# Longer runs of weight products: a whole weight chunk per run where it was one output tile

## The reference, cut to what matters

```
h = x
layer 0: h += moba_nsa_mixer(rmsnorm(h)) @ w_out ;  h += relu(rmsnorm(h) @ w1)**2 @ w2
layer 1: h += fox_mixer(rmsnorm(h))     @ w_out ;  h += relu(rmsnorm(h) @ w1)**2 @ w2
h = rmsnorm(h)
h += 0.5*rmsnorm(swiglu(rmsnorm(h)))                 # ffn1, width 2816
h += rmsnorm([diff_attention, ssd_mixer] @ w_out_2)  # mixer
h += 0.5*rmsnorm(swiglu(rmsnorm(h)))                 # ffn2
```

## Time and profile before

| | us |
|---|---|
| median of 3 runs | 1223.89 (1222.49 to 1224.58) |
| profiled execution | 1224.94 |
| its span in the profile | 1223.1 |
| PE busy | 1189.3 (97%) |
| PEld busy | 1052.5 (86%) |
| DVE busy | 825.5 (67%) |
| ACT busy | 658.4 (54%) |
| POOL busy | 239.4 (20%) |

### The profile page before, as it was taken

One profiled execution on the slowest core, in us unless ns is written; L12 is line 12 of the kernel. 1 busy time (PEld: TensorE's weight loads), 2 busy tenths in 40 slices (PEclk: granted clock), 3 DMA queues, 4 the chain that ended last, 5 costly groups with the idle time before them and its releaser, 6 DMA issues.

```text
span 1223.1 us, 19217 instructions
## 1 busy us (share of the span) xinstructions
PE 1189.3 (97%) x7770; PEld 1052.5 (86%) x7770; DVE 825.5 (67%) x1267; ACT 658.4 (54%) x1074; POOL 239.4 (20%) x300
## 2 busy tenths in 40 slices
PE   6899999999999999999999999999999999999996
PEld 6786788888888788888888889999997799888996
DVE  6957776666586686666568776457965767777643
ACT  6428666643333766664446555335546755665531
POOL 4105422110000341120112222000003711212101
PEclk9999999999999999999999999999999999999998
DMA  7790254555453435555544554562462122555451
GB/s 284 247 252 36 90 186 174 205 207 196 150 207 136 176 138 183 196 178 224 185 174 170 185 194 152 199 236 100 147 229 79 36 96 88 200 202 176 164 194 54
DMA packets 33800, 205.56 MB, mean 168 GB/s; under 512 B 3744, under 2 KB 6320, under 8 KB 12720
## 3 DMA queue, kind: packets, MB, share of 16 engines
q1 hardware_dynamic: 30416, 200.47, 45.3%
q10 hardware_dynamic: 3296, 3.87, 1.5%
HBM read 202.87 MB, written 1.46 MB: 167 GB/s over the span
## 4 chain that ended last, share of the span: by engine, by line
PE 85%; DVE 10%; ACT 3%; issue 1%; DMA 1%; POOL 0%; POOLq 0%; ACTq 0%
PE ps L667 38%; PE ps L671 20%; PE ps L683 5%; PE ps L685 5%; PE ps L684 5%; DVE wl L612 3%; PE ps L705 1%; PE ps L706 1%; PE ps L707 1%; DVE tf L2261 1%; PE ps L928 1%; PE ps L2577 1%; PE ps L2556 1%; DVE y L1982 1%; PE ps L1779 1%
## 5 line engine op out<-in xcount | busy, mean ns | idle before, releaser
L612 DVE TENSOR_TENSOR wl<-raw,wh 128x2048 fp32r<-128x2048 f32 (+2 forms) x194 | 420.7, 2174 | 141.8 <-ACT wh L583 141.7
L583 ACT ACTIVATE wh<-raw 128x2048 fp32r<-128x2048 f32 (+2 forms) x196 | 351.8, 1798 | 145.8 <-PE ps L671 63.8
L667 PE MATMUL ps<-xb,wh 128*128 128x512 f32 x1424 | 372.1, 393 | 0.0
L667 PEld LDWEIGHTS ps<-xb,wh 128*128 128x128 f32 x1424 | 257.2, 189 | 48.0 <-issue 0.6
L671 PE MATMUL ps<-xb,wl 128*128 128x256 f32 x1424 | 219.0, 282 | 2.3 <-DVE wl L612 1.4
L671 PEld LDWEIGHTS ps<-xb,wl 128*128 128x128 f32 x1424 | 201.8, 190 | 15.4 <-DVE wl L612 1.7
L667 PE MATMUL ps<-ab,wh 128*128 128x512 f32 x640 | 158.6, 392 | 0.1
L878 DVE TENSOR_TENSOR tf<-ps,tf 128x256 f32<-128x256 f32 x148 | 62.0, 422 | 116.0 <-ACT tf L873 115.9
L667 PEld LDWEIGHTS ps<-ab,wh 128*128 128x128 f32 x640 | 117.4, 188 | 23.5 <-DVE ab L994 0.8
L873 ACT ACTIVATE tf<-ps 128x256 f32<-128x256 f32 x148 | 56.4, 383 | 148.2 <-PE ps L671 144.6
L683 PE MATMUL ps<-ab,wh 128*128 128x256 f32 x448 | 127.5, 285 | 0.0
(11 more groups left out here) (328 smaller groups left out, 1557.3 us busy)
## 6 DMA issues: line engine op xcount, KB each, us to landing
raw<-wstream SPq DMA_DIRECT2D x162, 1024.0 KB, 4.8
raw<-wstream SPq DMA_DIRECT2D x32, 704.0 KB, 4.1
e_bt<-scratch ACTq DMA_DIRECT2D x16, 128.0 KB, 8.0
o_bt<-scratch SPq DMA_DIRECT2D x2, 1024.0 KB, 9.8
raw<-wstream SPq DMA_DIRECT2D x2, 560.0 KB, 7.9
raw<-wstream SPq DMA_DIRECT2D x4, 256.0 KB, 6.6
h<-xt ACTq DMA_DIRECT2D x4, 256.0 KB, 7.7
raw<-wstream SPq DMA_DIRECT2D x2, 512.0 KB, 9.6
```

Of the source, the lines that this page charges most:

```text
L583: e.g.activation(WH[i % HLN][:, 0:w], RAW[i % RAWN][:, 0:w], ACT.Copy).then_inc(S["hi"], 1)
L612: e.g.tensor_tensor(WL[q][:, 0:w], RAW[i % RAWN][:, 0:w], f32(WH[q][:, 0:w]), ALU.subtract).then_inc(S["lo"], 1)
L667: e.g.matmul(two(o[:, :]), WH[c % HLN][:, at * 128:at * 128 + 128], x2[:, :, tile(ks[k])], start=k == 0, stop=False, skip_group_check=True)
```

## The change

`pe_cols` groups the blocks by `(chunk, split)` instead of `(n, chunk, split)`. In a split group all wides of the chunk come first, then all its narrows; the wait for a tile's bank moves to the block with k = 0. The three kinds of steps become functions. The threefold matmuls keep their order.

```diff
-            for (n, c, split), blocks in groupby(p.blocks[part], lambda block: (block[0], block[2], p.split(block[0]))):
+            def wide(n, k, c, at):
+                if k == 0:
+                    e.wait(p.free[p.unit(n)])
+                e.wait_ge(S["hi"], stream_no(c, at))
+                ready(e, ks[k])
+                e.g.matmul(two(PS[p.bank[p.unit(n)]][:, :]), WH[c % HLN][:, at * 128:at * 128 + 128],
+                           x2[:, :, tile(ks[k])], start=k == 0, stop=False, skip_group_check=True)
+
+            def narrow(n, k, c, at):
+                e.wait_ge(S["lo"], stream_no(c, at))
+                return e.g.matmul(PS[p.bank[p.unit(n)]][:, 256:512], WL[c % HLN][:, at * 128:at * 128 + 128],
+                                  xh[:, tile(ks[k])], start=False, stop=k == p.nk - 1, skip_group_check=True)
...
+            for (c, split), blocks in groupby(p.blocks[part], lambda block: (block[2], p.split(block[0]))):
                 blocks = list(blocks)
...
                 if split:
...
+                    for n, k, _, at, _, _ in blocks:
+                        wide(n, k, c, at)
+                for n, k, _, at, _, signals in blocks:
+                    ins = (narrow if split else threefold)(n, k, c, at)
+                    if signals:
+                        ins.then_inc(S["gemm"], 1)
+                    if k == p.nk - 1:
+                        done += 1
+                        if after and done == p.after:
+                            after(e)
```

More of the change, by code:

```diff
@@ new lines, in narrow, with threefold @@
+            def narrow(n, k, c, at):
+                e.wait_ge(S["lo"], stream_no(c, at))
+                return e.g.matmul(PS[p.bank[p.unit(n)]][:, 256:512], WL[c % HLN][:, at * 128:at * 128 + 128],
+                                  xh[:, tile(ks[k])], start=False, stop=k == p.nk - 1, skip_group_check=True)
+            def threefold(n, k, c, at):
+                if k == 0:
+                    e.wait(p.free[p.unit(n)])
+                o = PS[p.bank[p.unit(n)]][:, 256 * (n % 2):256 * (n % 2) + 256]
+                wh, wl = pe_chunk(e, c, at)
+                ready(e, ks[k])
+                sl, cs = slice(at * 128, at * 128 + 128), tile(ks[k])
+                pair = n < special
+                start = k == 0 and (n % 2 == 0 or not pair)
+                e.g.matmul(o, wh[:, sl], xh[:, cs], start=start, stop=False, skip_group_check=pair)
+                e.g.matmul(o, wh[:, sl], xl[:, cs], start=False, stop=False, skip_group_check=pair)
+                return e.g.matmul(o, wl[:, sl], xh[:, cs], start=False, stop=k == p.nk - 1, skip_group_check=pair)
@@ L659, in pe_cols @@
+            for (c, split), blocks in groupby(p.blocks[part], lambda block: (block[2], p.split(block[0]))):
                 blocks = list(blocks)
-                o = PS[p.bank[p.unit(n)]]
-                if blocks[0][1] == 0:
-                    e.wait(p.free[p.unit(n)])
                 if split:
[L664 to L691, removed]
+                    for n, k, _, at, _, _ in blocks:
[8 more added lines that the diff above has]
+                            after(e)
```

## The result

The changed kernel takes 1218.98 us (median of 5 runs, 1217.81 to 1219.90) against 1223.89 (5 runs); ratio 0.9958, 95% interval 0.9947 to 0.9968. It is 4.9 us faster; 4.5 were forecast (1219.4). Beside later kernels on another occasion it took 1219.26 (5 runs, 1218.81 to 1220.26) against 1223.91: 4.65 us, ratio 0.9962 (0.9948 to 0.9976).

A forecast was written before the change was run, and what follows sets the result against it. PE was taken to bound the kernel, busy 97% of the span, with DVE setting the time before 75 us. 1.66 + 0.4 + 2.9 - 0.48 = 4.5 us from the median 1223.89 gives 1219.4; range 1217.2 to 1222.8.

The forecast's parts named there:

- pace of the repeated chunks: In 83 chunks after 75 us, runs of sixteen instead of eight save 0.020 us each: 1.66 us.
- first chunks after the attention: First chunks of up0, oq, ok, up1 and gate1, until now wide and narrow in turn, save 0.08 us each: 0.4.
- early waits: In the first chunks of qm and qn, sixteen wides cover PE's wait for the weight rest: 2.9 us gained in all.
- tails of eo and oo: Behind each attention, block 6's two narrows come after the wait for block 7: 0.24 us lost twice, 0.48 in all.
- the bank step in the middle: Changed runs pass between banks midway; if that cost as much as a switch, nothing of the 1.66 us would be left.
- The row of down0: Two chunks of down0, already in runs of sixteen, took 5.565 us each against 5.585 in up0; used to price the pace.
- The cap: At ev0, DVE must finish a rest before freeing the bank ks's first tile leaves; limits the 3.0 us lead to 2.9.
- No load could hold it back: In the attention, no load under way in 89.6 to 96.5 us (DMA share 0.00), so the 2.9 us lead is kept.
- Cover at k = 7: In first chunks PE reaches k = 7's wides earlier; hidden by 0.8 us in up0, 0.3 in gate1; counted 0.
- The slower rival: In gate1 and gate2, bunched drains make DVE's round exceed 5.57 us a chunk: about 1228 us; chance 0.05.
- 7 us of stored lead: In the slower gate1 and gate2 case, subtracted from 16 us of excess over 41 chunks to reach about 1228 us.
- The clock: With PE 2.9 us early, the clock's fall at 89.6 to 96.5 may change: some 2 us either way; worse case chance 0.03.

The follow-up runs named there:

- qm_first: Kernel before with the new grouping only in the first chunk of qm: 1223.07 us against 1224.19, ratio 0.9989.
- qn_first: Kernel before with the new grouping only in the first chunk of qn: 1222.26 us against 1224.19, ratio 0.9985.
- early_first: Kernel before with the new grouping only in the first chunks of qm, km, qn and ks: 1220.96 us against 1223.91, ratio 0.9967.
- tail_old: Changed kernel with the first chunks of eo and oo in the old order: 1219.31 us, beside 1219.26 for the changed kernel and 1223.91 before.
- pace_only: Kernel before with the new grouping in every chunk but the first of each product: 1222.29 us against 1223.91, ratio 0.9986.
- runs_of_32: Changed kernel with down0 and down1 in runs of 32, a whole output tile: 1232.14 us against 1224.21 for the kernel before, ratio 1.0059.

## Why the prediction was right, point by point

| term | forecast, us | in the traces, us |
|---|---|---|
| pace of the repeated chunks | 1.66 | 0.020 in each of 80 chunks, 1.6; alone 1.6 in the runs |
| first chunks after the attention | 0.4 | 0.18 |
| early waits | 2.9 | 2.92; alone 2.95 in the runs |
| tails of eo and oo | -0.48 | -0.50 |
| sum | 4.5 | 4.1 to 4.3 without the clock's part; 4.9 and 4.65 in the runs |

The forecast is right in its three main mechanisms, and each was run alone. But the traces give 0.2 to 0.4 us less than the 4.5, and the medians 0.2 to 0.4 us more, so that 4.5 lies so near to both is partly luck. Why the medians show more than the traces isn't settled: the interval of the ratio alone is 2.6 us wide.

- *Pace.* Right, 5.587 to 5.567 us, and the bank step in the middle is free. The row of down0 was the right price. Three of the 83 chunks, those behind PE's sums, gain nothing. My account beside it, "what half of the switches cost", was wrong as a law: twos are cheaper than eights. It was a price for one step, from eight to sixteen, and no slope.
- *First chunks.* The mis-sized term. up0, up1 and gate1 gave 0.084 each (5.652 to 5.568 us). oq and ok lost 0.035 each (5.632 to 5.667, 5.655 to 5.689): their pairs had run at quicker rhythms (230 and 117 ns in oq), and I had set them equal to up0's. Wides alternating between two banks cost no more than in one.
- *Early waits.* 1.1 and 1.6 to 1.7 us at the two places, DVE's stretch moved as one block, and the lead lived through the attention: each shown, by `qm_first`, `qn_first` and `early_first`. The cap that I put on it wasn't seen. PE's chunks alone give the 2.92, and PE never waited for DVE's late drain of ks, so the 0.1 that the cap took from 3.0 was right by luck.
- *No load could hold it back.* This step was wrong. The stretch that I read, 89.6 to 96.5, begins 1.3 us after the last bias load had landed, so its empty DMA share says nothing of that load. With a lead of 2.9 it landed late in one of two profiles of the changed kernel and cost PE 0.54 us of lead. A larger lead would leave it less room.
- *Tails.* Right at both places.
- *Cover at k = 7.* Right: in up0 and gate1 the first chunks ran 16 wides without a gap (5.568 us).
- *Gate stages.* The slower rival had no part. The bunching is there, but POOL's step no longer takes 1.55 us: 0.95 of that ran beside DVE's weight rest, and in the new order the rest is over before. I had moved it with its old length. (The "7 us of stored lead" in that rival's sum stands on no row.) Timelines of POOL and DVE in the changed kernel:

```profile
701.45 0.74 POOL L1852 TENSOR_TENSOR tf<-sg,tf 128x256 f32<-128x256 f32 x1 [4.83 <-ACT sg L1817]
```

```profile
702.00 0.43 DVE L884 TENSOR_TENSOR tf<-ps,tf 128x256 f32<-128x256 f32 x1 [0.47 <-ACT tf L879]
702.53 0.69 DVE L1878 TENSOR_TENSOR tf<-tf,rb 128x512 f32<-128x512 f32 x1
```

  It ends at 702.19, before DVE asks for it at 702.53. Nothing slips.
- *The clock.* Given as 2 us either way, on top. In the first profile it gave 3.3 us against before's, more than that. (2 us below the forecast is 1217.4; the range was stated from 1217.2.) The run of sixteen that I had expected near 138.2 began at 136.16 for that reason, and near 138.2 in `tail_old`, whose fall was as long as before's.
- *The gap between matmuls.* The formula that the prediction took from the Trainium skill ("TensorE: Matmul & The Clock Gate", section "Back-to-back issue gap") is given there for the isolated gap. The same section says that in a stream of weight loads and matmuls both set the spacing. In this stream the steady gaps are 227 and 120 ns, 11 above the formula. It has no term for the order, and by it the sum would have been without its pace. The 1.6 us of `pace_only` and the positions above speak against that in this kernel.

## What to carry to other kernels

Group matmuls so that everything that needs only the early operand comes first; the gain is largest where the late operand's engine is busy without a break, and it can be priced from one trace as "chunk with wait less chunk without". A longer run eats the cover at its start and holds its operand buffers longer: go only as far as the inputs at the start of a product and the number of buffers allow (sixteen was free here, thirty-two lost 13 us). For edits worth a few us, compare starts of the same matmul at stage edges and take the clock's falls out before believing a span.

## What the runs showed that I had not expected

- The clock's falls make 1 to 3 us between executions of one kernel, and each shows only as a jump of the lead. 3.4 us at the low level cost 0.8 to 1.4 us in the attention and the mixer, and 1.5 to 1.6 in dense work (`runs_of_32`).
- POOL's 128x256 operation in gate1 and gate2 takes 0.74 us where no weight rest of DVE runs beside it, and else 0.60 us plus all the time that it shares with the rest: 1.15 to 2.67 us in 38 of 44 cases before. After the change 5 of 44 meet a rest, and POOL's busy time fell from 239.4 to 218.2 us over the kernel.
- A load of 128 KB, issued 2.8 us earlier than before, landed 2.0 us later, after 20.0 us instead of 15.3. Nothing here shows why.
- The same order of single pairs runs at two paces, 347 and 353 ns a pair.
